# Heads 0 to 5 of the second mixer's output projection: three output tiles moved from the output phase into the last head

## The reference, cut to what matters

```python
proj = h @ w_in                        # q, k, v, z of 8 heads (4 x 128 columns each), and two gates
conv = silu(short convolution of q, k, v)
o, S = gated_delta_rule(q, k, v, g, beta, S0)
o = rms_norm(o, o_norm) * silu(z)      # head by head
y = o.reshape(B, T, HV) @ w_out        # 1024 x 1024: the sum over the 8 heads
...
hp = hp + yp                           # the residual
hp = hp + swiglu(rms_norm(hp, norm_ffn), w_gate_up, w_down)
```

## Time and profile before

| | us |
|---|---|
| median of 3 runs | 1359.73 (1357.37 to 1360.74) |
| profiled execution, whole | 1358.81 |
| its span | 1356.9 |
| head 5, with 32 parts filled in | 43.76 |
| head 6, with 28 parts | 45.96 |
| head 7, with 11 parts | 42.28 |
| output phase, with 57 parts | 39.48 |

### The profile page before, as it was taken

How to read it: one execution, slowest core, us unless ns; L and a number is a source line. 1 busy time by engine, 2 the same in 40 slices (tenths; PEclk the granted TensorE clock), 3 DMA queues, 4 the chain that set the end, 5 groups by cost and what they waited for, 6 DMA issues and landing times.

```text
span 1356.9 us, 28034 instructions
## 1 busy us (share of the span) xinstructions
PE 1318.8 (97%) x11596; PEld 1091.7 (80%) x11596; DVE 640.6 (47%) x1019; ACT 508.1 (37%) x785; POOL 368.8 (27%) x504
## 2 busy tenths in 40 slices
PE   8999899999999999999999999988999999999997
PEld 6766588888888888877788777865888888888886
DVE  5447653333333233366877787764433333333222
ACT  5234443222322232253655455544433222232231
POOL 1005224121221110254454454442121212221010
PEclk9999999999999999998999999998999999999999
DMA  8568422422223322201121222020322232233211
GB/s 265 200 201 272 128 94 94 170 94 106 93 93 116 129 86 75 91 32 62 64 78 49 94 63 95 33 78 32 141 94 93 93 111 96 102 116 118 96 43 64
DMA packets 32140, 140.90 MB, mean 104 GB/s; under 512 B 4633, under 2 KB 6937, under 8 KB 20154
## 3 DMA queue, kind: packets, MB, share of 16 engines
q1 hardware_dynamic: 32058, 139.75, 29.5%
HBM read 128.63 MB, written 11.11 MB: 103 GB/s over the span
## 4 chain that ended last, share of the span: by engine, by line
PE 92%; DVE 5%; issue 1%; ACT 1%; DMA 0%; SPq 0%; DVEq 0%
PE P L1684 64%; PE P L2063 10%; PE P L2218 2%; PE P L2203 1%; PE P L2280 1%; PE P L2072 1%; PE P L2211 1%; DVE arena L1425 1%; PE P L2078 1%; PE P L2246 1%; PE P L2260 1%; PE P L1781 1%; PE P L1913 1%; PE P L2230 1%; PE P L2236 1%
## 5 line engine op out<-in xcount | busy, mean ns | idle before, releaser
L1684 PE MATMUL P<-zh,wh 128*128 128x260 f16 x1712 | 329.2, 273 | 2.4 <-DVE wl L1163 2.4
L1684 PE MATMUL P<-zl,wh 128*128 128x260 f16 x1712 | 329.0, 273 | 0.0
L1684 PE MATMUL P<-zh,wl 128*128 128x260 f16 x1712 | 329.0, 273 | 0.0
L1143 DVE SCALAR_TENSOR_TENSOR wl<-stage,wh 128x2048 f16<-128x2048 f32 (+1 forms) x76 | 187.3, 2465 | 198.3 <-ACT wh L751 195.9
L1684 PE MATMUL P<-arena,wh 128*128 128x260 f16 x1832 | 278.5, 273 | 0.7 <-DVE hT L1360 0.4
L1684 PEld LDWEIGHTS P<-arena,wh 128*128 128x128 f16 x1832 | 176.9, 97 | 28.9 <-issue 1.4
L1684 PEld LDWEIGHTS P<-zh,wh 128*128 128x128 f16 x1712 | 164.3, 97 | 34.1 <-issue 7.9
L1684 PEld LDWEIGHTS P<-zh,wl 128*128 128x128 f16 x1712 | 165.6, 97 | 25.9
L1684 PEld LDWEIGHTS P<-zl,wh 128*128 128x128 f16 x1712 | 165.4, 97 | 25.8
L1684 PE MATMUL P<-arena,wl 128*128 128x260 f16 x916 | 176.0, 273 | 0.0
L751 ACT ACTIVATE wh<-stage 128x2048 f16<-128x2048 f32 (+1 forms) x82 | 165.6, 2019 | 3.6 <-PE P L1684 3.6
(11 more groups left out here) (361 smaller groups left out, 1652.9 us busy)
## 6 DMA issues: line engine op xcount, KB each, us to landing
stage<-w_gu SPq DMA_DIRECT2D x44, 1024.0 KB, 4.8
stage<-w_in SPq DMA_DIRECT2D x23, 1024.0 KB, 5.0
stage<-w_dn SPq DMA_DIRECT2D x16, 1408.0 KB, 5.8
arena<-cache_k SPq DMA_DIRECT2D x32, 256.0 KB, 3.4
stage<-w_out SPq DMA_DIRECT2D x8, 1024.0 KB, 6.6
arena<-cache_v SPq DMA_DIRECT2D x32, 256.0 KB, 3.0
arena<-delta_state SPq DMA_DIRECT2D x8, 512.0 KB, 3.5
o_ds<-arena SPq DMA_DIRECT2D x8, 512.0 KB, 6.9
```

The source lines that it names most:

```text
L1143: nc.vector.scalar_tensor_tensor(out=wl[:, j, 0:words], in0=stage[:, j, 0:words], scalar=WS, in1=wh[:, j, 0:words], op0=MUL, op1=SUB).then ...
L1684: mm = nc.tensor.matmul(pm[j][:, c, :], w[:, wslot, o:o + 128], x[:, k, c * CH:(c + 1) * CH], start=(k == first and w is wh and x is xh), ...
```

## The change

The 64 parts of `out1` are dealt out anew.

- Head 6 fills all 32 parts of head 7's projection, as the other heads do, and its `leave(7, 3)` is at its end.
- Head 7 fills 25 parts of `out1` (`early_part`): output tiles 0, 1 and 2 over heads 0 to 5 (`EARLY_K` = 6), and tile 3 over heads 0 to 6. All go to `pm[0]`. DVE adds tiles 0, 1 and 2 to `hT` as they are (`leave_early`, semaphores `part_done` and `part_free`).
- POOL copies the blocks of heads 6 and 7 of unit 0 (both tiles, `wh` and `wl`) to `tailw`, so that slot 0 is free: unit 2 is loaded by SPq in the step of head 6, split by ACT in level 5 of head 7 and by DVE in quarters in its chunk stage. Unit 3 is loaded in the same step of SPq.
- The output phase (`output_rest`) takes tile 4 from unit 2 in `pm[1]`, with `stat_last` in it, and head 7 of tile 3; then heads 6 and 7 of tiles 2, 0 and 1; then tiles 5, 6 and 7. `OUT_ROWS` is that order. DVE adds what comes to `hT`, a second time for tiles 0 to 2.

```diff
-OUT1_CALLS = (3, 4, 5, 6, 7, 9, 11)
+EARLY, EARLY_K = 3, 6
+OUT_ROWS = (3, 4, 2, 0, 1, 5, 6, 7)
...
+        tailw = ddt.bitcast(f16).rearrange("p (m k n c) -> p m k n c", m=2, k=KD - EARLY_K, n=2)
...
-                    elif u < 18:
+                    elif u < 20:
                         weights(w_out1, FIRST_UNIT["in1"] + u, u % 2, u - 16, WORDS[FIRST_UNIT["in1"] + u])
...
-            stream(w_out1, "out1", skip=2)
...
+                else:
+                    pool.wait_ge(hi_ready, FIRST_UNIT["out1"] + 1)
+                    pool.wait_ge(lo_ready, FIRST_UNIT["out1"] + 1)
+                    for m, w in enumerate((wh, wl)):
+                        nc.gpsimd.tensor_copy(tailw[:, m].rearrange("p k n c -> p (k n c)"),
+                                              w[:, 0, 256 * EARLY_K:256 * KD]).then_inc(tail_saved, 1)
...
+                            u = FIRST_UNIT["out1"] + 2
+                            act.wait_ge(part_done, 2)
+                            act.wait_ge(tail_saved, 2)
+                            act.wait_ge(w_in[0], 16 * (u // 2 + 1))
+                            split_rest("out1", 0)
                 if p < HG:
...
-            project_out("out1", 3)
+            for at in range(KD):
+                norm_tile(3, at, "out1")
+                if at == 2:
+                    act.wait_ge(mm_done, FIRST_TILE["out1"] + 3)
+                    act.wait_ge(w_in[1], 16 * (FIRST_UNIT["out1"] // 2 + 2))
+                    split_rest("out1", 1)
+                if at == 5:
+                    next_split("out1", 1, 0)
+                if at == 7:
+                    next_split("out1", 1, 1)
...
+            def leave_early(t):
+
+                dve.wait_ge(part_done, t + 1)
+                nc.vector.scalar_tensor_tensor(out=paired(hT[:, t, :]), in0=pm[0], scalar=1 / WS,
+                                               in1=paired(hT[:, t, :]), op0=MUL, op1=ADD).then_inc(part_free, 1)
+
+            def leave_out(at):
+                k = OUT_ROWS[at]
+                dve.wait_ge(mm_done, FIRST_TILE["out1"] + at + 1)
+                nc.vector.scalar_tensor_tensor(out=paired(hT[:, k, :]), in0=pm[at % 2], scalar=1 / WS,
+                                               in1=paired(hT[:, k, :]), op0=MUL, op1=ADD).then_inc(pm_free, 1)
+
...
-                if p == HG:
-                    leave(h, 3)
...
                 if p < HG:
                     leave(p, 0)
+                else:
+                    leave_early(0)
...
+                        else:
+                            leave_early(1)
...
+                else:
+                    leave_early(2)
...
-                        if p < HG and c == 1:
+                        if c == 1:
...
-                        if p < HG and c == 2:
+                        if c == 2:
...
-                        if p < HG:
-                            split_quarter(FIRST_UNIT["in1"] + 2 * p + 2, 0, 0)
+                        split_quarter(FIRST_UNIT["in1"] + 2 * p + 2, 0, 0)
...
-                if p < HG - 1:
+                if p < HG:
                     leave(p, 3)
...
-            project_out("out1", 3)
+            leave_out(0)
+            leave_out(1)
+            norm_lo(3, OUT_ROWS[0], 0)
+            leave_out(2)
+            norm_lo(3, OUT_ROWS[1], 1)
+            leave_out(3)
+            norm_lo(3, OUT_ROWS[2], 2)
+            leave_out(4)
+            split_lo(FIRST_UNIT["out1"] + 3, 1, WORDS[FIRST_UNIT["out1"] + 3])
+            norm_lo(3, OUT_ROWS[3], 3)
+            norm_lo(3, OUT_ROWS[4], 4)
...
+            for at in range(6, KD):
+                leave_out(at)
+                norm_lo(3, OUT_ROWS[at], at)
+            next_split("out1", 1, 1)
...
+            def early_part(i):
+
+                t, k = divmod(i, EARLY_K) if i < EARLY * EARLY_K else (EARLY, i - EARLY * EARLY_K)
                 if k == 0:
-                    pe.wait_ge(hi_ready, FIRST_UNIT["out1"] + 1)
-                    pe.wait_ge(lo_ready, FIRST_UNIT["out1"] + 1)
-                    pe.wait_ge(pm_free, FIRST_TILE["out1"])
+                    pe.wait_ge(hi_ready, FIRST_UNIT["out1"] + t // 2 + 1)
+                    pe.wait_ge(lo_ready, FIRST_UNIT["out1"] + t // 2 + 1)
+                    if t == 0:
+                        pe.wait_ge(pm_free, FIRST_TILE["out1"])
+                    else:
+                        pe.wait_ge(part_free, t)
                 pe.wait_ge(m1_lo, k + 1)
-                product(0, 0, 0, mh1, ml1, KD, 256, (k,))
+                mm = product(0, t // 2, 128 * (t % 2), mh1, ml1, EARLY_K if t < EARLY else KD, 256, (k,))
+                if t < EARLY and k == EARLY_K - 1:
+                    mm.then_inc(part_done, 1)
...
+            def output_tail(j, n):
+
+                for k in range(EARLY_K, KD):
+                    for m, x in ((0, mh1), (0, ml1), (1, mh1)):
+                        for c in range(2):
+                            mm = nc.tensor.matmul(pm[j][:, c, :], tailw[:, m, k - EARLY_K, n, :],
+                                                  x[:, k, c * CH:(c + 1) * CH],
+                                                  start=(k == EARLY_K and m == 0 and x is mh1),
+                                                  stop=(k == KD - 1 and m == 1))
+                return mm
...
+            def output_rest():
+
+                base, t = FIRST_UNIT["out1"], FIRST_TILE["out1"]
+                pe.wait_ge(hi_ready, base + 3)
+                pe.wait_ge(lo_ready, base + 3)
+                pe.wait_ge(*G("s", 4 * HG))
+                product(1, 0, 0, mh1, ml1, KD, 256, range(1))
+                stat_last()
+                product(1, 0, 0, mh1, ml1, KD, 256, range(1, HG - 1))
+                pe.wait_ge(m1_lo, HG)
+                product(0, 1, 128, mh1, ml1, KD, 256, (HG - 1,)).then_inc(mm_done, 1)
+                product(1, 0, 0, mh1, ml1, KD, 256, (HG - 1,)).then_inc(mm_done, 1)
+                pe.wait_ge(pm_free, t + 1)
+                product(0, 1, 0, mh1, ml1, KD, 256, range(EARLY_K, KD), first=EARLY_K).then_inc(mm_done, 1)
+                pe.wait_ge(pm_free, t + 2)
+                output_tail(1, 0).then_inc(mm_done, 1)
+                pe.wait_ge(pm_free, t + 3)
+                output_tail(0, 1).then_inc(mm_done, 1)
+                pe.wait_ge(pm_free, t + 4)
+                product(1, 0, 128, mh1, ml1, KD, 256).then_inc(mm_done, 1)
+                unit("out1", 1, 1, mh1, ml1)
...
-                    first = 28 if h == HG - 1 else 0
-                    last = 28 if h == HG - 2 else 32
-                    for part in range(first + done[0], min(first + done[0] + n, last)):
-                        project_part(min(h + 1, HG - 1), part)
+                    last = EARLY * EARLY_K + HG - 1 if h == HG - 1 else 32
+                    for part in range(done[0], min(done[0] + n, last)):
+                        if h == HG - 1:
+                            early_part(part)
+                        else:
+                            project_part(h + 1, part)
                         done[0] += 1
-                    if h == HG - 1 and done[0] >= 4:
-                        calls[0] += 1
-                        if calls[0] in OUT1_CALLS:
-                            output_part(OUT1_CALLS.index(calls[0]))
...
-                fill(4)
+                fill(4 if h < HG - 1 else 3)
...
-                fill(2)
+                fill(2 if h < HG - 1 else 1)
...
-                    fill((1, 1, 1, 1, 1, 2)[l])
+                    fill((1, 1, 1, 1, 1, 2 if h < HG - 1 else 1)[l])
...
-                    fill((1, 1, 1, 1, 1, 2 if h == HG - 2 else 4)[l])
+                    fill((1, 1, 1, 1, 1, 4 if h < HG - 1 else 1)[l])
...
-                        fill(2 if h == HG - 2 else 3)
+                        fill(3)
...
-            phase_in_two("out1", mh1, ml1, HG - 1, len(OUT1_CALLS), stat_last, lambda k: pe.wait_ge(m1_lo, k + 1))
+            output_rest()
```

More of the change, by code:

```diff
@@ L1714, in phase @@
                         unit(name, i, j, xh, xl)
[L1716 to L1733 removed]
             def z_ready(b):
                 def wait(k):
[L1737 removed]
+                    pe.wait_ge(z_lo, KD * b + (k if b < 3 else max(OUT_ROWS.index(i) for i in range(k + 1))) + 1)
                 return wait
```

53 lines of the change are left out of this document (23 added, 30 removed).

## The result

The changed kernel takes 1344.16 us (median of 4 runs, 1341.62 to 1344.68) beside 1359.24 for the kernel before (4 runs): a ratio of 0.988, 95% interval 0.9858 to 0.9902, so it is faster by about 1.2%. The forecast was 1342.8, with the range 1340.0 to 1350.5. A second set of runs, in which the two were run again, gave 1342.87 us (4 runs) and 1360.43 (11 runs), 0.9875 (0.9842 to 0.9907). The profiled execution of the changed kernel took 1344.58 us (span 1342.4), that of before 1358.81: 14.2 us less, where the sum said 16.4.

A forecast was written before the change was run, and what follows sets the result against it. PE was taken to bound the output phase, chain latency head 7. From 1358.81 us, less 2.0 (head 6), 2.3 (head 7) and 12.1 (output phase), came 1342.4; with 0.9 to the median it said 1342.8, range 1340.0 to 1350.5.

The forecast's parts named there:

- the sum: Whole kernel: profiled 1358.81 us less 2.0 (head 6), 2.3 (head 7) and 12.1 (output phase) gives 1342.4 us.
- The price of a part where PE is full: Output phase: 38.23 us over 57 parts, so 0.67 us a part.
- Head 6: Head 6 with 32 parts gets shorter, as DVE's wait of 2.98 us goes: gain 2.0 us, ends 0 and 2.2.
- Room in head 7: Head 7, bound by its chain's latency, takes 14 parts more in its waits and still falls by 2.3 us to 40.0.
- The chunk stage: Head 7's chunk stage, 7 parts added, returns to full clock: 14.79 to 12.2 us, gain 2.6; ends -6.8 and 2.8.
- the thin levels ahead: Head 7: half clock in the chunk stage comes after three levels in which PE has had one part in all.
- rival 4: Slower than before: half clock from early in head 7 into the output phase, about 33 us to eat 16.4; chance 3%.
- The levels: Head 7, levels 0 to 5, with 12 parts instead of 6: cost 0 to 0.8 us, taken as 0.3.
- from level 4 on PE's own work sets the pace and takes the delay up: Head 7's levels: why the delay from DVE's addition of tile 1 was priced at 0.3 us, within 0 to 0.8.
- The start of the head: Head 7 up to level 0: 6 parts instead of 5, hidden in a 1.19 us wait for POOL's copy; cost 0.
- POOL's copies, ACT's split, SPq: Head 7's two POOL copies, ACT's split moved into level 5, and SPq's earlier loads: cost 0 each.
- Output phase: Loses 18 parts at 0.67 us, 12.1 us, to 27.4; nothing waits at the short tiles, bounds 0 and 3 us.
- rival 1: No room in head 7: added parts lengthen it; kernel 1346.2 us, or 1354.1 at full price; chance 12%.

The follow-up runs named there:

- the eleven traces: Profiled executions of kernels that leave head 0's code as it is; head 0 alone took between 47.37 and 52.65 us in them.

## Why the prediction was right, point by point

- **The price of a part where PE is full, 0.67 us**: right. 18 parts gave 12.12 us for 12.1, and 7 gave 4.70 for 4.7.
- **Head 6**: right in place and size, 2.21 us for 2.0. The edit alone gives it. POOL's q squares held nothing.
- **Room in head 7**: right, and the step that carried the forecast. 14 parts more made the head shorter. The rule of the Trainium skill that busy matmul time doesn't show the headroom (Perfetto Trace Analysis, Identifying the Most-Contended Engine) agrees with that: PE had 34.82 of 42.28 us busy, took 9.4 us more work, and the head fell to 40.66.
- **The chunk stage**: 2.46 us for 2.6, the mechanism half right. It was the clock, but my reason for its fall, the thin levels ahead, is only one of two, so that the number came out owes something to luck: the seven parts that I put in the stage were there for the output phase, not for the clock. Idle parts in the levels alone give 13.96 us, in the chunks alone 15.31, in both 12.40; the changed kernel has 12.33, and 12.82 without its parts there. And "half of it at half clock" misreads: a mean clock of 0.66 is half clock for two thirds of the 14.79 us, the 10 us that rival 4 reckons with.
- **The levels**: the mis-sized term. I had +0.3 us with 0.8 as the upper bound; it was +1.04. The parts cost 0.44, close to the 0.5 that I had worked out. What failed is the step "from level 4 on PE's own work sets the pace and takes the delay up". Nothing was taken up: levels 4 and 5 take 3.23 and 2.81 us, with idle parts and without the delay 3.17 and 2.78. I had also followed the addition to z and v alone, and not to the next tile's first part, which wants the same bank (0.41 us in level 3). The start of the head gave 0.20 us that I had at nothing; in all head 7 gained 1.62 us for 2.3.
- **POOL's copies, ACT's split, SPq**: no cost seen. The copies take 0.61 us each and the decay L728 starts at 929.39. ACT's split begins at 935.88 and the first chunk has no wait.
- **Output phase**: no stall at the short tiles, as laid out: the rows show no wait of PE over 0.15 us in the phase. That two `zl` would take 3.48 us wasn't foreseen; it met the slack.
- **The sum's own slips**: 1342.4 and the 0.9 us between execution and median are 1343.3, not 1342.8, and rival 1 is priced from 1342.4 where the others start at 1342.8. Neither moves the forecast by more than 0.5 us; the median measured was 1344.16.
- **Against the runs**: 16.4 us forecast, 15.95 in the stages, 14.2 between the two profiled executions, 15.1 between the medians. The difference behind the stages is for the most part head 0, where the changed kernel's execution happened to lose 1.28 us more (52.63 for 51.35) with its code unchanged. Over the eleven traces head 0 spreads by 5.3 us, which the prediction hadn't foreseen; that the median came within 1.4 us of the forecast is in part luck.

## What to carry to other kernels

Work moved from a stage that PE bounds into one that the latency of a chain bounds costs little there, and can give time back if pauses of PE had let the clock fall; test it with idle matmuls at the same places before writing the real move. Fill the pauses of the whole stretch: in the executions here parts on one side of it didn't keep the clock up on the other. And where work is moved into gaps of an engine that runs in order, ask for each piece what it waits for, a bank included: what stands behind it waits too. Read a single slow instruction against the other engines' rows at its end: eight columns that take 3.08 us and end with another engine's work are held, and moving that other work was worth more here than filling the pause.
